# Feed-forward of a fused two-block kernel: 12 of 22 gate/up tile pairs by seven block products instead of eight, in two parts of 11

## The reference, cut to what matters

```python
    for l in range(DEPTH):                      # DEPTH = 2
        ...
        x = x + merged @ w_o[l]
        h = rms_norm(x, g_ffn[l])
        x = x + (jax.nn.silu(h @ w1[l]) * (h @ w3[l])) @ w2[l]
```

## Time and profile before

| | |
|---|---|
| median of three runs | 3241.65 us (3241.46 to 3242.42) |
| span of the profiled execution | 3241.1 us |
| TensorE matmul busy | 3216.7 us, 99% |
| TensorE weight load busy | 2689.0 us, 83% |
| VectorE busy | 1801.7 us, 56% |
| ScalarE busy | 1305.7 us, 40% |
| GpSimd busy | 631.9 us, 19% |
| granted TensorE clock, mean | 0.999 |

### The profile page before, as it was taken

The page is one execution under the profiler, slowest core; times in us unless marked ns, Lnnn a source line. Parts: engine busy times, 40 slices in busy tenths (PEclk is TensorE's granted clock), DMA queues, the critical chain, the costliest instruction groups (busy, mean ns, idle before and its releaser), DMA issues.

```text
span 3241.1 us, 38219 instructions
## 1 busy us (share of the span) xinstructions
PE 3216.7 (99%) x15436; PEld 2689.0 (83%) x15436; DVE 1801.7 (56%) x2728; ACT 1305.7 (40%) x1991; POOL 631.9 (19%) x502
## 2 busy tenths in 40 slices
PE   9999999999999999999999999999999999999998
PEld 7888888888888888888888888888888898788887
DVE  6865775444348655845443465554544268974433
ACT  5653553333237534633322323332323248743221
POOL 1521241111005311520110022111111013521101
PEclk9999999999999999999999999999999999999999
DMA  4122323323221122332233222222223322223332
GB/s 137 48 74 68 108 89 104 101 98 102 93 93 59 60 78 87 109 94 94 95 101 103 96 81 81 82 91 92 93 97 97 99 85 93 93 92 100 97 98 85
DMA packets 85136, 295.60 MB, mean 91 GB/s; under 512 B 9568, under 2 KB 12128, under 8 KB 84960
## 3 DMA queue, kind: packets, MB, share of 16 engines
q1 hardware_dynamic: 84384, 292.76, 27.4%
q10 hardware_dynamic: 576, 0.40, 0.0%
HBM read 291.02 MB, written 2.10 MB: 90 GB/s over the span
## 4 chain that ended last, share of the span: by engine, by line
PE 87%; DVE 7%; ACT 3%; issue 1%; POOL 1%; DMA 1%; SPq 0%; ACTq 0%; DVEq 0%; POOLq 0%
PE bank L313 86%; PE bank L316 2%; DVE wl L569 2%; ACT m_p L536 1%; DVE small L1304 1%; DMA raw<-in_wts 1%; ACT wh L533 1%; POOL u_g L591 1%; DVE u_uc L565 0%; DVE m_ptl L569 0%; DVE c_kl L569 0%; DVE m_qf L559 0%; ACT m_pth L533 0%; DVE u_t L565 0%; DVE m_sh L809 0%
## 5 line engine op out<-in xcount | busy, mean ns | idle before, releaser
L569 DVE TENSOR_TENSOR wl<-raw,wh 128x1024 fp32r<-128x1024 f32 (+1 forms) x531 | 661.1, 1248 | 760.7 <-ACT wh L533 759.8
L313 PE MATMUL bank<-zh,wh 128*128 128x512 f32 (+1 forms) x2652 | 1025.0, 386 | 6.1 <-ACT zh L533 6.1
L313 PE MATMUL bank<-zh,wl 128*128 128x512 f32 (+1 forms) x2652 | 1019.9, 385 | 1.9 <-DVE wl L569 1.9
L313 PE MATMUL bank<-zl,wh 128*128 128x512 f32 (+1 forms) x2652 | 1018.3, 384 | 2.2 <-DVE zl L572 2.1
L533 ACT ACTIVATE wh<-raw 128x1024 fp32r<-128x1024 f32 (+1 forms) x531 | 555.8, 1052 | 534.8 <-PE bank L313 468.6
L313 PEld LDWEIGHTS bank<-zh,wl 128*128 128x128 f32 x2652 | 498.6, 188 | 107.4 <-DVE wl L569 7.2
L313 PEld LDWEIGHTS bank<-zh,wh 128*128 128x128 f32 x2652 | 499.0, 188 | 102.3 <-ACT zh L533 6.1
L313 PEld LDWEIGHTS bank<-zl,wh 128*128 128x128 f32 x2652 | 499.0, 188 | 98.6 <-DVE zl L572 3.7
L313 PE MATMUL bank<-f_mh,wh 128*128 128x512 f32 (+1 forms) x748 | 285.2, 381 | 0.0
L313 PE MATMUL bank<-f_mh,wl 128*128 128x512 f32 (+1 forms) x748 | 283.3, 379 | 0.0
L313 PE MATMUL bank<-f_ml,wh 128*128 128x512 f32 (+1 forms) x748 | 280.8, 375 | 0.0
(11 more groups left out here) (337 smaller groups left out, 4471.2 us busy)
## 6 DMA issues: line engine op xcount, KB each, us to landing
raw<-in_wts SPq DMA_DIRECT2D x529, 512.0 KB, 3.3
c_nb<-in_c_bias SPq DMA_DIRECT2D x16, 384.0 KB, 3.2
x<-in_xT SPq DMA_DIRECT2D x8, 256.0 KB, 5.9
out<-x SPq DMA_DIRECT2D x13, 128.0 KB, 1.8
b_mask<-in_b_mask SPq DMA_DIRECT2D x2, 576.0 KB, 4.4
r_d<-in_decay SPq DMA_DIRECT2D x4, 256.0 KB, 2.7
raw<-in_wts SPq DMA_DIRECT2D x2, 256.0 KB, 3.7
m_t<-in_mla_tab SPq DMA_DIRECT2D x2, 256.0 KB, 4.8
```

Of the source, the lines that this page charges most:

```text
L313: return self.e.matmul(out, l, r, start=start, stop=stop, skip_group_check=inside)
L569: return self.e.tensor_tensor(out, src, b32(hi), ALU.subtract)
```

## The change

Each layer's feed-forward is done in two parts of HALF = 11 units. After units 0 to 10 comes a first pass of `w2` over their 11 tiles (eight output tiles in banks 0 to 7, added to x by eight more VectorE additions); after units 11 to 21 a second pass over the other 11, added as before. The kinds of the units are written out: U is a unit as before; N is a plain unit on the activations with norm and gain already applied; S is a unit by seven products.

An S unit sees gate and up tile as a 2 x 2 block problem: K in two halves of four tiles, tokens in two halves of 256, gate and up as the two columns. Instead of eight block products (four K tiles each, 256 tokens) it makes seven, of sums of blocks. A product is 4 tiles x 3 matmuls of 256 columns. The unit's weights become four pieces: three chunks of 1024 columns (two products each) and one of 512 (one product). Two of the pieces are sums, made by VectorE out of the raw weights (`sums`: one 128x1024 and one 128x512 addition; `low_s`: one more 128x512 addition). The last piece of unit i is used by TensorE only after the first piece of unit i+1 (or, when an N unit follows, after that unit's first chunk; or at once, when none follows).

The activations' side: `vector_normed_x` makes x times gain times rrow (eight operations on 128x512), split into `nh`, `nl` (eight copies, eight low parts); four sums of token halves and K halves (`n_t`, four 128x1024 additions) are split into `th`, `tl` (four copies, four low parts of 128x1024), which lie over zh and zl and so wait for the last U unit.

Weights have four raw buffers between the first N unit and the second pass of w2 (two pairs; an S unit takes a pair), two elsewhere. At the switch to four buffers the chunk in hand is closed. Three loads of tables for the next layer (m_t, b_rc, b_rs) move from events early in the feed-forward to the end of the first pair of the second w2 pass.

```diff
+HALF = 11
+KINDS = "UUUUNNSSNSS" + "SSNSSNSSNSS"
...
+    def product(self, w, side, x, k0, out, fresh, *event):
+        for k in range(4):
+            cs = slice(512 * side + 128 * k, 512 * side + 128 * k + 128)
+            xh, xl = x(k0 + k)
+            self.wait_ge("wh", *w[3])
+            self.mm(out, w[1][:, cs], xh, fresh and k == 0, False, True)
+            self.mm(out, w[1][:, cs], xl, False, False, True)
+            self.wait_ge("wl", *w[3])
+            t = self.mm(out, w[2][:, cs], xh, False, k == 3, True)
+        t.then_inc(*self.tell("mm", event, *self.spent(w)))
...
     def split(self, c):                      # VectorE
+        after = self.book.s_next(c)          # is the next piece the first of an S unit?
+        if after:
+            self.sums(*after[2:])
+        if self.book.ring[c][0] == "s":
+            self.low_s(c, *self.book.ring[c][1:])
+            return
...
+    def sums(self, unit, a, b):
+        m = self.m
+        src = m.s_raw[self.book.loads[a][0] // 2]
+        landed(self, a)
+        landed(self, b)
+        if self.free_b:
+            self.wait_ge("wl", *self.free_b)
+        self.tt(m.s_b, src[:, 0:1024], src[:, 512:1536], ALU.add).then_inc(*self.tell("wl", "S1", *unit))
+        self.wait_ge("wl", "S1", *unit)
+        self.tt(src[:, 512:1024], m.s_b[:, 512:1024], src[:, 0:512], ALU.add).then_inc(*self.tell("wl", "S2", *unit))
...
+def tensor_unit(L, F, l, i, tail):
...
+    w = L.s_chunk(0, unit, loads)
+    a = L.claim(A, "cp", "g1", *unit)[:, 0:256]
+    L.product(w, 0, normed_quarter(L, F, 0), 0, a, True, "P1", *unit)
+    b = L.claim(B, "ev", "s2", *unit)[:, 0:256]
+    L.product(w, 1, token_sum(L, F, 1), 0, b, True, "P6", *unit)
+    tail()
+    w = L.s_chunk(2, unit, loads)
+    c = L.claim(C, "ev", "u6", *unit)[:, 0:256]
+    L.product(w, 0, token_sum(L, F, 2), 0, c, True, "P7", *unit)
+    d = L.claim(D, "ev", "g2", *unit)[:, 0:256]
+    L.product(w, 1, token_sum(L, F, 0), 0, d, True, "P5", *unit)
+    w = L.s_chunk(3, unit, loads)
+    L.wait_ge("cp", "s1", *unit)
+    L.product(w, 0, normed_quarter(L, F, 0), 4, a, False, "P2", *unit)
+    def last():
+        w = L.s_chunk(1, unit, loads)
+        L.wait_ge("ev", "s3", *unit)
+        L.product(w, 0, token_sum(L, F, 3), 0, c, False, "Q4", *unit)
+        L.wait_ge("ev", "u7", *unit)
+        L.product(w, 1, normed_quarter(L, F, 1), 4, d, False, "P3", *unit)
+    return last
...
+def scalar_units(L, F, l, units):
+    for i in (*units, None):
...
+        if i is not None and KINDS[i] == "S":
+            scalar_s1(L, F, i)               # copy P1 (128x256)
+        if not first and KINDS[prev] == "S":
+            scalar_unit_gate(L, F, prev)     # tanh, needs g2 of prev
+        if not first:
+            scalar_half_mid(L, F, l, prev)   # high part, needs GpSimd's product
+        if i is not None and KINDS[i] == "N":
+            scalar_unit_gate(L, F, i)
+        if i is not None and KINDS[i] == "S":
+            scalar_g1(L, F, i)               # copy P1+P2, needs P2
+        L.ahead()
+def vector_units(L, F, units):
+    for i in (*units, None):
...
+        if i is not None and KINDS[i] == "S":
+            vector_s2(L, F, i)               # needs P6
+        if not first and KINDS[prev] == "S":
+            vector_unit_out(L, F, prev)      # g2, u6: need P3, Q4 of prev
+            vector_unit_gate(L, F, prev)     # needs tanh of prev
+        if i is not None and KINDS[i] == "S":
+            vector_s3(L, F, i)               # s3 needs P7, u7 needs P5
+        if not first:
+            vector_half_mid(L, F, prev)      # low part
+        if i is not None and KINDS[i] == "N":
+            vector_unit_gate(L, F, i)
+        L.ahead()
...
 def vector_ffn1(L, l):
-    vector_mids(L, ("f", l))
+    L.lead = 2
+    vector_normed_x(L, F, l)
+    for i in range(first):                   # the four U units
+        vector_mid_in(L, F, i, 0, unit_banks(i))
+        vector_mid_in(L, F, i, 1, unit_banks(i))
+        if i:
+            vector_half_mid(L, F, i - 1)
+        if i < 2:
+            vector_normed(L, F, range(4 * i, 4 * i + 4))
+        vector_mid_gate(L, F, i)
+        if i == 1:
+            vector_token_sums(L, F)
+        L.ahead()
+    for j in T_ORDER:
+        vector_token_sum(L, F, j)
+        L.ahead()
+    vector_units(L, F, range(first, HALF))
```

More of the change, by code:

```diff
@@ L71, in __init__, with s_next, needs @@
         self.plan, self.turns, self.mark = [], {}, {}
+        self.ring, self.loads = [], []
+    def s_next(self, c):
+        c += 1
+        return self.ring[c] if c < len(self.ring) and self.ring[c][0] == "s" and self.ring[c][1] == 0 else None
+    def needs(self, c):
+        c = min(c, len(self.ring) - 1)
+        after = self.s_next(c)
+        return max([r[-1] for r in self.ring[max(0, c - 8):c + 1]] + ([after[-1]] if after else []))
 class Dry:
@@ L183, in __init__ @@
         o = 4096
-        self.raw = [self.place(f"raw{i}", o + 1024 * i, 1024) for i in range(RAWS)]
+        self.s_raw = [self.place("s_raw0", o, 1024 * RAWS)]
+        self.raw = [self.s_raw[0][:, 1024 * i:1024 * i + 1024] for i in range(RAWS)]
         o += 1024 * RAWS
@@ L343, in skip, with s_loads, s_chunk @@
         self.pos = 8
+    def s_loads(self):
+        self.skip()
+        self.slot = (self.slot + self.slot % 2) % self.slots
+        return [self.load() for _ in range(2)]
+    def s_chunk(self, part, unit, loads):
+        self.skip()
+        self.chunk += 1
+        self.level, self.next, self.pos = self.chunk, self.chunk + 1, 8
+        self.book.ring.append(("s", part, unit, *loads))
+        c, s = self.chunk, self.chunk % RING
+        return c, self.m.wh[s], self.m.wl[s], (c,)
+    def product(self, w, side, x, k0, out, fresh, *event):
[8 more added lines that the diff above has]
+        t.then_inc(*self.tell("mm", event, *self.spent(w)))
     def spent(self, w):
@@ L603, in __init__, with load @@
         self.loaded, self.inside = 0, False
-    def load(self, c):
+    def load(self, n):
         m = self.m
[L607 to L610, removed]
+        slot, after = self.book.loads[n]
+        if after:
+            self.wait_ge(*after)
+        self.e.dma_start(m.raw[slot], m.A["wts"][n]).then_inc(*self.tell(f"raw{slot}", n, by=16))
     def weights(self, upto, least=-1):
-        while not self.inside and self.loaded <= min(max(upto + 2, least), self.book.chunks - 1):
+        while not self.inside and self.loaded <= self.book.needs(max(upto + 2, least)):
             self.inside = True
@@ new lines, in nothing, with tensor_units @@
+def nothing():
+    pass
+def tensor_units(L, F, l, units):
+    tail = nothing
+    for i in units:
+        if KINDS[i] == "N" and L.slots == RAWS:
+            L.use_slots(4, ("mm", "acc") + F + (0, 0))
+        if KINDS[i] == "S":
+            tail = tensor_unit(L, F, l, i, tail)
+        else:
+            n = [F + (w, i) for w in range(2)]
+            x = L.z_whole() if KINDS[i] == "U" else normed(L, F)
+            L.group(n, 8, x, w13_desc, unit_banks(i), [("ev",) + y for y in n], {3: tail})
+            tail = nothing
+    tail()
@@ L2227, in scalar_ffn1 @@
+    scalar_units(L, F, l, range(first, HALF))
+    scalar_units(L, F, l, range(HALF, FF))
     if l:
@@ L2247, in gpsimd_ffn1 @@
     gpsimd_stat(L, ("ffn", l))
-    gpsimd_mids(L, ("f", l))
+    for i in range(FF):
+        gpsimd_unit(L, ("f", l), i)
     if l == 0:
@@ L3544, in numbered @@
         book.turns = pe.turn
-    book.chunks = len(book.plan)
+    book.chunks = len(book.ring)
     return book
```

340 lines of the change are left out of this document (313 added, 27 removed).

## The result

The changed kernel takes 3283.53 us, the median of four runs (3282.3 to 3284.97), against 3241.56 us (3241.41 to 3242.42) for the kernel before: 1.0128 times as long, with a 95% interval of 1.0113 to 1.0142. The prediction was 3270 us (3238 to 3290) and slower. The profiled execution spans 3280.6 us where the sum gave 3269.7, so 10.9 of the 13.5 us are to be explained in the trace, besides where the predicted part really lies. The rest is that the median lies 2.9 us above this span, and the forecast added 0.55.

A forecast was written before the change was run, and what follows sets the result against it. TensorE's matmuls were taken to bound the kernel (87% of the chain). 3241.1 - 23.6 + 2 x (4.45 + 3.2) + 1.0 + 22.7 + 6.2 + 7.0 = 3269.7 us of span, plus 0.55: 3270 us, range 3238 to 3290.

The forecast's parts named there:

- A: Start of the feed-forward stage: copy and low part of weight chunk r7 come late, 4.45 us a layer.
- C: Behind the second of two successive S units: next piece's copy and low part late, 1.63 or 2.41 us; 22.7 both layers.
- D: N unit between pairs of S units: load, weight sums and low part end late, 0.77 x 8 = 6.2 us.
- E: Pair of S units behind such an N unit: D's lateness carries on, 0.88 x 8 = 7.0 us.
- Rival 1: Weight splits keep ahead inside the S units, so C, D and E cost nothing: 3234.4 us, chance 0.15.
- gain: S units: 84 matmuls of 256 columns at 0.1178 us, 9.90 us a unit against 10.88; 23.6 us won in both layers.
- B: Token sums after unit 3: their chain makes chunk r11's low part late, 3.2 us a layer.
- B': Second layer's first S unit: its second half lands in the buffer that r11 frees, 3.3 us later; 1.0 us once.
- Rival 4: After the stalls of A and B TensorE's clock may be 1.2 GHz: +15, about 3285 us, chance 0.06.
- main case: The case of the sum, gain against A to E: 3270 us, own range 3256 to 3284, chance 0.62.
- At nothing: Extra additions to x, moved table loads and w2's matmuls put at no cost; 11 us if w2's cover were gone.
- Rival 3: The loads in D collide and take 5.3 us: 2.0 x 8 more, 3286 us, chance 0.13.

The follow-up runs named there:

- experiment 1: Changed kernel with ScalarE's weight copy for the piece behind a pair's second S unit moved ahead of the high part that waits for GpSimd: 3259.29 us.
- experiment 2: Changed kernel with the copies and low parts of three weight chunks (r7, r8, r11) put earlier in both queues, around the token sums: 3271.87 us.
- experiment 8: As experiment 5, but 9 S units a layer in place of 12, none next to another within a part: 3232.02 us.
- experiment 9: Changed kernel with no move, only 9 S units a layer, none next to another within a part: 3250.45 us.
- experiment 6: As experiment 5, with VectorE's third weight addition put behind the following chunk's low part, except where the unit's last piece follows at once: 3248.43 us.
- experiment 7: Changed kernel with the edits of experiment 2 and experiment 3 and all 18 later units plain N units, no S unit: 3250.58 us.
- experiment 5: Changed kernel with the edits of experiment 1, experiment 2 and experiment 3 together: 3242.29 us.
- experiment 10: As experiment 5, with the three weight additions made over 64 columns, the first of a layer whole, waits and order kept: 3231.0 us.
- experiment 3: Changed kernel with VectorE making a plain chunk's low part before the two weight sums, where an S unit's first piece follows: 3286.94 us.

## Why the prediction was right, and where its sizes were off

**Sign and mechanism.** The change made the kernel slower because copies and low parts come late in fixed queues. Experiments 1 and 2 show it for A and C, each by taking away a lateness without removing work; D and E are a matter of VectorE's work, see below. Rival 1 (C to E nothing) is what experiments 8 and 9 nearly make true with fewer pairs; with the changed kernel's own kinds and order it isn't. That the sum of A to E came so near is in part luck: A was put 2.0 us too low, while C and E came 0.9 and 1.6 us smaller than forecast.

**The terms**, both layers, in us:

| term | predicted | measured |
|---|---|---|
| gain | 23.6 | 21.6 |
| A | 8.9 | 10.9 |
| B | 6.4 | 5.8 |
| B' | 1.0 | 0.9 |
| C, pairs with a unit behind them | 8 x 1.63 = 13.0 | 8 x 1.55 = 12.4 |
| C, pairs with none | 4 x 2.41 = 9.6 | 4 x 2.35 = 9.4 |
| D | 6.2 | 5.9 |
| E | 7.0 | 5.4 |
| reduced clock | 0 | about 6.4 |
| N units on the normed activations | 0 | 1.3 |

The measured stalls sum to 50.7, against 52.2 predicted. Over the two feed-forwards -21.6 + 50.7 + 6.4 + 1.3 gives 36.8 us, and they are 41.0 us longer. The 4.2 us left would be 0.08 us for each of the 52 waits of the list above; the one restart shown in experiment 6 costs 0.10. The rest of the program takes back 1.5. So the 10.9 us between the sum and the span lie in what was put at nothing (6.4, 1.3, and these 4.2) and in the gain (2.0), less 1.5 outside the stage and 1.5 by which A to E together are smaller than forecast.

**Gain.** An S unit has 48 matmuls over z at 0.1200 and 36 on the normed activations at 0.1178, of which the first 12 of a pair mostly run at 0.1133: 9.98 us on average, against 9.90 from the earlier trace rows, and 0.90 x 24 = 21.6. The mis-sized step is "the same three-matmul pattern on ready operands": over z the same pattern took 2 ns more. Similarly N units run at 0.2289 a matmul against 0.2267, 0.11 us x 12. Both differences go with the operands in the rows; whether it is their place was not tried apart. Where an S unit stands alone, 24 of its matmuls run at 0.1178 and 12 at 0.1133, 9.95 us; an N unit of 48 x 0.2289 = 10.99 less this is 1.04. Experiments 7 and 8 gave 1.03 by the medians, and 0.92 by the traces, or 1.00 without the waits at the first S units.
The Trainium skill (TensorE: Matmul & The Clock Gate, Back-to-back issue gap) gives N/2.4 + 2.5 ns for the isolated gap, 0.109 at 256 columns. No distance here is as low: 0.1133 is the least.

**A.** The step that failed is "GpSimd's product of unit 1 waits for the first of them". It waited for both additions, 3.31 us. The prices of the lock itself held: 1.11 after the VectorE operation's end against the 1.14 of the earlier trace rows.
The Trainium skill (SBUF — State Buffer, "SBUF: two separate sides") says that whoever starts first gets the shared port pair for the whole instruction. The trace agrees for one operation; it adds that a waiting GpSimd did not get its turn between two VectorE operations that followed at once.

**Clock.** Rival 4 came true in part, beside the main case: 6.4 us instead of its 15, after A in both layers and after two stalls of C, not after B. The step that failed is "Clock: 1.00 throughout". Experiment 2 shows the link: with A's rest gone the clock stays at 1.00 there. In kernels 5, 6, 7, 8 and 10, whose longest rest in the stage is 0.87 us, it stays at 1.00 through both feed-forwards.

**D and E.** Their sizes were nearly right. The prediction worked them out as lateness carried on from chunk to chunk, which starts with the weight sums that wait for a load. Experiments 3 and 6 show that an exchange of order only moves the wait, experiment 5 that VectorE has work without a gap over about the first 12 us of such a pair, and experiment 10 that leaving out most of the sums removes the waits. Rival 1's count, 25 us of VectorE in 30.7 of TensorE, was an average over three units; at the start of the two S units there is no slack (experiment 5).

**At nothing.** Eight more additions to x and the moved table loads cost nothing that shows: between the two parts TensorE has no wait in kernel 7. Rival 3 (slow loads in D) didn't come: between 640 and 800 us the median load takes 3.4 us and the longest 4.9, and D is 0.46 to 1.27.

**Experiment 3's time.** It came out 3.4 us above the changed kernel with slightly less waiting (42.6 us against 44.0 for low parts, copies and `s3`, counted as in the list of waits). Its mean clock is 0.995 against 0.997. In the first layer the clock fell after B as well, and after both last stalls of C, where it hadn't in the changed kernel:

```profile
630.00:645.00 15.00, 12.52 (x41) 9.41 (x41) 10.67 (x13) 6.59 (x8) 0.00 (x0) 0.77 0.21 71
```

That layer's feed-forward takes 6.1 us longer than in the changed kernel, the second layer's, with less reduced clock, 4.1 us shorter. So the clock is enough to explain the difference.

**Open.** Why the clock fell after some rests and not after others. After A's rest of 4.67 to 4.69 us it fell in both layers of every kernel that has it; after rests of 1.9 to 2.35 us it fell in one layer or kernel and not in another.

## What to carry to other kernels

Price an algorithm with fewer matmuls by the fullest stretch of the engine that pays for it, not by its average: here each seven-product pair is worth about 1 us when it stands alone and a third of that in twos. When every engine runs a queue in fixed order, look for a prefetch that stands behind a wait for a slower engine; here the moves of experiments 1 and 2 alone gave back 24.2 and 11.7 us, and they add no work. A long stall may be charged again by the clock after it; here each rest of A was.

## What the hardware showed that was not expected

- A GpSimd addition of 1.29 us took 3.31 us beside two VectorE additions of 1.22 us back to back; it got no turn between them.
- The distance of matmuls at 256 columns was 0.1200, 0.1178 or 0.1133 us, and at 512 columns 0.2267 or 0.2289, at clock 1.00, differing with the operands and, at 256 columns, with what ran before.
- Around and after a rest of 4.67 us the granted clock was 0.74 over 13 us (605 to 618 us); around one of 2.13 us in experiment 2, 0.83 over 10 us in the first layer, and 1.00 over 15 us (1565 to 1580) at the same rest of the second.
- A stall costs about 0.1 us beyond its length, since the matmul behind the late one follows at 0.22 us in place of 0.12 (790.21 - 789.99 in experiment 6).
